# Modulation tiles among the gate groups, cosines from a magnitude, and a new order of low halves and head loads

## The reference, cut to what matters

```
# first block
proj = rms_norm(x) @ w_in                 # q, k, v, u, gate_a, gate_b
y_a  = windowed attention(q, k, v) @ w_attn_o
y_b  = state-space scan over u, both directions, then a gated linear unit (glu)
x    = x + (sigmoid(gate_a) * y_a + sigmoid(gate_b) * y_b) @ w_out
# experts: every token picks 8 x 16 of 16384 single-neuron experts
x    = x + sum over picked experts of weight * gelu(h . down[e]) * up[e]
# second block, for layer 0 and 1
shift, scale, gate = split(silu(c) @ w_mod[layer] + b_mod[layer], 3)      # and the same for c_ctx
x_in = x * (1 + scale) + shift
layer 0: short convolution and 8 latent attention heads;  layer 1: grouped attention
```

## Time and profile before

| | us |
|---|---|
| median of three runs | 4051.4 |
| the runs | 4050.02 to 4071.21 |
| the profiled execution | 4045.63 |
| its span | 4043.8 |
| TensorE's mean granted clock in it | 0.987 |

### The profile page before, as it was taken

The page is one execution under the profiler, slowest core; times in us unless marked ns, Lnnn a source line. Parts: engine busy times, 40 slices in busy tenths (PEclk is TensorE's granted clock), DMA queues, the critical chain, the costliest instruction groups (busy, mean ns, idle before and its releaser), DMA issues.

```text
span 4043.8 us, 73486 instructions
## 1 busy us (share of the span) xinstructions
PE 3846.4 (95%) x30344; PEld 3566.3 (88%) x30344; DVE 2409.5 (60%) x3400; ACT 1673.4 (41%) x2349; POOL 818.0 (20%) x599
## 2 busy tenths in 40 slices
PE   6999998899999988999999999999999999989997
PEld 6767677799999987999999999999799997778887
DVE  6999976543677767555555555533333333657556
ACT  4223345544455567333444334432222223243674
POOL 4878763234400000000000000000000002113223
PEclk9999999999999999999999999999999999999999
DMA  5777773245455544555655555522522223214323
GB/s 218 300 305 276 302 283 133 108 180 185 168 191 193 195 140 137 190 197 188 225 221 217 194 201 194 191 105 95 175 91 86 104 104 125 94 66 143 116 104 135
DMA packets 141589, 695.06 MB, mean 172 GB/s; under 512 B 44256, under 2 KB 54624, under 8 KB 61664
## 3 DMA queue, kind: packets, MB, share of 16 engines
q1 hardware_dynamic: 89952, 641.77, 43.2%
q10 hardware_dynamic: 51456, 50.74, 3.7%
HBM read 672.54 MB, written 19.92 MB: 171 GB/s over the span
## 4 chain that ended last, share of the span: by engine, by line
PE 77%; DVE 14%; ACT 3%; issue 3%; DMA 1%; POOL 1%; ACTq 0%; DVEq 0%; SPq 0%; POOLq 0%
PE banks L422 50%; PE banks L2231 17%; DVE w_lo L400 2%; PE banks L2299 1%; DVE pq L1340 1%; DVE banks L1330 1%; PE banks L2142 1%; PE banks L2401 1%; ACT w_hi L392 1%; DVE rq L1376 1%; DVE banks L1317 1%; DVE oh L1577 1%; PE banks L2467 1%; PE banks L2442 1%; POOL w_lo L400 1%
## 5 line engine op out<-in xcount | busy, mean ns | idle before, releaser
L422 PE MATMUL banks<-h_hi,w_hi 128*128 128x256 f32 (+1 forms) x6176 | 1640.7, 287 | 62.4 <-DVE w_lo L400 30.8
L422 PE MATMUL banks<-h_hi,w_lo 128*128 128x256 f32 (+1 forms) x6176 | 1617.3, 283 | 0.0
L422 PE MATMUL banks<-h_lo,w_hi 128*128 128x256 f32 (+1 forms) x6176 | 1616.9, 283 | 0.0
L392 ACT CAST w_hi<-ring 128x1024 fp32r<-128x1024 f32 x986 | 984.4, 1048 | 1041.3 <-PE banks L2231 427.5
L400 DVE TENSOR_TENSOR w_lo<-ring,w_hi 128x1024 fp32r<-128x1024 f32 x806 | 1000.8, 1274 | 559.7 <-ACT w_hi L392 555.2
L422 PEld LDWEIGHTS banks<-h_hi,w_hi 128*128 128x128 f32 x6176 | 1110.7, 189 | 126.3 <-issue 98.5
L422 PEld LDWEIGHTS banks<-h_hi,w_lo 128*128 128x128 f32 x6176 | 1109.4, 189 | 13.2 <-issue 0.5
L422 PEld LDWEIGHTS banks<-h_lo,w_hi 128*128 128x128 f32 x6176 | 1109.1, 189 | 11.8
L400 POOL TENSOR_TENSOR w_lo<-ring,w_hi 128x1024 fp32r<-128x1024 f32 x180 | 460.3, 2557 | 1628.9 <-ACT w_hi L392 1627.4
L2231 PE MATMUL banks<-wp_hi,w_hi 128*128 128x256 f32 x2048 | 566.3, 277 | 5.2 <-DVE wp_lo L1610 5.1
L2231 PE MATMUL banks<-wp_hi,w_lo 128*128 128x256 f32 x2048 | 566.1, 276 | 0.0
(11 more groups left out here) (388 smaller groups left out, 4307.3 us busy)
## 6 DMA issues: line engine op xcount, KB each, us to landing
ring<-in_stream_dram SPq DMA_DIRECT2D x555, 1024.0 KB, 4.8
spare<-in_stream_dram SPq DMA_DIRECT2D x30, 1024.0 KB, 5.9
cst<-in_stream_dram SPq DMA_DIRECT2D x23, 1024.0 KB, 6.7
g_in<-g_out ACTq DMA_DIRECT2D x8, 1024.0 KB, 6.4
g_out<-stage ACTq DMA_DIRECT2D x31, 256.0 KB, 2.6
hb<-heads_d ACTq DMA_DIRECT2D x8, 768.0 KB, 6.7
heads_d<-stg ACTq DMA_DIRECT2D x4, 1024.0 KB, 8.7
X<-in_x_in_dram SPq DMA_DIRECT2D x2, 1024.0 KB, 7.1
```

The source lines that it names most:

```text
L392: act.copy(w_hi[:, t.par, s], weights(t.slot)[:, s]).then_inc(hi_done, 1)
L422: m = pe.matmul(bank(b, e - a, a), w[:, t.par, k], x(k)[:, a:e], start=first and a == 0, stop=last and e == n, skip_group_check=e - a < n)
```

## The change

- Four modulation tiles an octet, 32 in all, leave the mixed stage and form the phase `gmod` behind `down0`. They run between the gate groups, one a group and two at four of them (`late_by`), with eight turns; their input and their copy use the place of constants that are loaded again afterwards. For that the gate groups use three sets of two banks, and bank 7 and 6 serve the late tiles. The groups' loops are written out.
- Cosines: VectorE rounds one phase only; ScalarE takes its magnitude and then the cosine as the sine of a quarter turn less the magnitude. The coefficients' last two instructions become one.
- Gate projections: GpSimd makes both low halves. Glu: VectorE makes both; the high split goes ahead of the exponentials, the first low half ahead of the wait for them.
- First up tile: its splits come behind the gate groups.
- Head loop: values are loaded by themselves; queries, keys and rotated queries of the next head are loaded once the present scores have been read.

```diff
-PHASES = [("u", 8), ("v", 4), ("mix", 136), ("gate", 12), ("glu", 16), ("attno", 16),
+PHASES = [("u", 8), ("v", 4), ("mix", 104), ("gate", 12), ("glu", 16), ("attno", 16),
-          ("down0", 64), ("up0", 64), ("down1", 64), ("up1", 64),
+          ("down0", 64), ("gmod", 32), ("up0", 64), ("down1", 64), ("up1", 64),
-SLOTS = [(D_, M_, M_), (M_, M_), (D_, M_), (D_, M_), (M_, M_), (D_, M_), (D_, M_), (M_, M_)]
+SLOTS = [(D_, M_), (M_,), (D_, M_), (D_, M_), (M_,), (D_, M_), (D_, M_), (M_,)]
+LATE = 16
-LAST = {4: G0["gate"], 5: G0["mix"] + MIX * 6 + 4, 6: G0["mix"] + MIX * 4 + 11}
+LAST = {4: G0["gate"], 5: G0["mix"] + MIX * 6 + 3, 6: G0["mix"] + MIX * 4 + 9}
...
-            b = 2 * (n % 4)
+            b = 2 * (n % 3)
+        def late_by(n):
+            return min(32, 32 * (n + 1) // 28)
...  ScalarE: tables
-                act.wait_ge(S("phs_ready"), c0 + 1)
-                act.activation(tab[c0 % 2][:], ph[:, 0:2], ACT.Sin, scale=TURN).then_inc(S("tab_ready"), 1)
+                act.wait_ge(S("phs_ready"), 2 * c0 + 1)
+                act.activation(ph[:, 1], ph[:, 0], ACT.Abs).then_inc(S("phs_ready"), 1)
+                act.wait_ge(S("phs_ready"), 2 * c0 + 2)
+                act.activation(tab[c0 % 2][:, 0], ph[:, 0], ACT.Sin, scale=TURN)
+                act.activation(tab[c0 % 2][:, 1], ph[:, 1], ACT.Sin, bias=V("halfpi"), scale=-TURN)\
+                    .then_inc(S("tab_ready"), 1)
...  ScalarE: glu
                 t = Tile("glu", h)
+                hi_split(act, t.next())
                 act.wait_ge(S("negmax_ready"), h + 1)
...
-                hi_split(act, t.next())
...  ScalarE: gate groups
-            with act.Fori(0, 7, 1) as i:
-                for n in range(4, 8):
-                    gates_weigh(n, i, 4)
-                    gates_stage(n - 2, i, 4)
-                    gates_store(n - 3, i, 4)
+            def late_out(b):
+                act.wait_ge(mm_done, Tile("gmod", 4 * (b - LATE) + 3).done())
+                act.wait_ge(S("mod_turned"), b)
+                act.copy(mtmp_late, bank(7)).then_inc(S("mod_out"), 1)
+            for n in range(2, 32):
+                gates_weigh(n)
+                gates_stage(n - 2)
+                if n >= 3:
+                    gates_store(n - 3)
+                while blocks < 24 and late_by(n - 1) >= 4 * (blocks - LATE + 1):
+                    late_out(blocks)
+                    blocks += 1
+            hi_split(act, Tile("up0", 0))
...  ScalarE: head loop
+                act.dma_start(hb[:, 0:2].unsqueeze(1), of_head(i)[:, :, 0:2]).then_inc(S("head_loaded"), 16)
...
+                act.dma_start(hb[:, 2:3].unsqueeze(1), of_head(i)[:, :, 2:3]).then_inc(S("values_loaded"), 16)
...
+                if more:
+                    scores_load(i + 1)
...  GpSimd
             for j in range(12):
-                lo_split(pool, Tile("gate", j).next(), 0)
-            for j in range(16):
-                lo_split(pool, Tile("glu", j).next(), 0)
+                for h_ in (1, 0):
+                    lo_split(pool, Tile("gate", j).next(), h_)
...  VectorE: phases and coefficients
-                L(dve.tensor_scalar(ph[:, 1], ph[:, 0], 0.25, None, ALU.add))
-                for f in range(2):
-                    L(dve.tensor_scalar(ph[:, 2], ph[:, f], MAGIC, MAGIC, ALU.add, ALU.subtract))
-                    m = dve.tensor_tensor(ph[:, f], ph[:, f], ph[:, 2], ALU.subtract)
+                L(dve.tensor_scalar(ph[:, 2], ph[:, 0], MAGIC, MAGIC, ALU.add, ALU.subtract))
+                dve.tensor_tensor(ph[:, 0], ph[:, 0], ph[:, 2], ALU.subtract).then_inc(S("phs_ready"), 1)
...
-                L(dve.tensor_tensor(ph[:, 0], ph[:, 0], ph[:, 1], ALU.add))
-                dve.tensor_scalar(co[:, :, 2], ph[:, 0], -1.0, None, ALU.mult).then_inc(S("c_made"), 1)
+                dve.scalar_tensor_tensor(co[:, :, 2], ph[:, 0], -1.0, ph[:, 1], ALU.mult, ALU.subtract)\
+                    .then_inc(S("c_made"), 1)
...  VectorE: gates, glu
-                lo_split(dve, Tile("gate", j).next(), 1)
...
+                lo_split(dve, t.next(), 1)
                 dve.wait_ge(S("exp_done"), h + 1)
...
-                lo_split(dve, t.next(), 1)
+                lo_split(dve, t.next(), 0)
...  VectorE: gate groups
+            for n in range(2, 32):
+                onehots(n)
+                scale(n - 2)
             scale(30)
             scale(31)
+            for h in (1, 0):
+                lo_split(dve, Tile("up0", 0), h)
...  TensorE
-                if v in (0, 2, 5) and q:
+                if v in (0, 5) and q:
                     pe.wait_ge(S("mix_read"), d)
                     mod_turn(q // 4 - 1)
...
-                    pe.wait_ge(S("gates_in"), g(-3))
-                    pe.wait_ge(S("g_staged"), g(-3))
+                    pe.wait_ge(S("gates_in"), g(-2))
+                    pe.wait_ge(S("g_staged"), g(-2))
...
+            def late_tile(j):
+                t = Tile("gmod", j)
+                if j % 4 == 0:
+                    pe.wait_ge(S("mod_out"), LATE + j // 4)
+                pe.wait_ge(tile_loaded[t.slot], t.loaded())
+                for r in range(4):
+                    m = pe.matmul(banks[32 * r:32 * r + 32, 7, :], csp_late[:, 4 * (j % 4) + r], weights(t.slot)[:, 4 * r:4 * r + 4],
+                                  start=(j % 4 == 0), stop=(j % 4 == 3))
+                m.then_inc(mm_done, 1)
+            for n in range(32):
                 gates_pe(n)
+                if turned < 24 and made >= 4 * (turned - LATE + 1):
+                    late_turn(turned)
+                    turned += 1
+                while made < late_by(n):
+                    if made % 4 == 0 and made // 4 + LATE > turned:
+                        late_turn(turned)
+                        turned += 1
+                    late_tile(made)
+                    made += 1
```

More of the change, by code:

```diff
@@ L725, in _ @@
             act.activation(sv[:], sv[:], ACT.Exp).then_inc(S("sel_acts"), 1)
-            with act.Fori(0, 16 - SELECT, 1) as i:
+            with act.Fori(0, 15 - SELECT, 1) as i:
                 for j in range(4):
@@ L730, in _ @@
                     down_act(t, i * 4 + (j + 4 * SELECT))
+            for j in range(60, 64):
+                t = Tile("down0", j)
+                if j < 63:
+                    hi_split(act, t.next())
+                down_act(t, j)
             act.sem_inc(S("sel_acts"), 1)
@@ L778, in _ @@
             gates_store(31)
+            act.wait_ge(S("mod_turned"), 24)
+            act.copy(modf[:, 8 * LATE:], bank(6, 64)).then_inc(S("mod_read"), 1)
             act.dma_start(C("rm"), consts[:, CONST["rm"][0]:CONST["rm"][0] + 1024]).then_inc(S("back"), 16)
             act.dma_start(C("rg"), consts[:, CONST["rg"][0]:CONST["rg"][0] + 512]).then_inc(S("back"), 16)
-            up_act(0)
+            for j in range(4):
+                hi_split(act, Tile("up0", j).next())
+            up_act(0, 1)
             act.wait_ge(mm_done, G0["down1"])
@@ L898, in _, with of_head, scores_load @@
             act.wait_ge(S("head_loaded"), 16)
[L900 to L904 removed]
+            def of_head(i):
+                return heads_d.rearrange("h p a t -> p h a t")[:, bass.ds(i, 1)]
+            def scores_load(i):
+                act.dma_start(hb[:, 0:2].unsqueeze(1), of_head(i)[:, :, 0:2]).then_inc(S("head_loaded"), 16)
                 for half in range(2):
@@ L907, in _, with conv_head @@
                                   rope_d.rearrange("h p t -> p h t")[:, bass.ds(i, 1)]).then_inc(S("head_loaded"), 16)
+            def conv_head(i, more=True):
+                tb, tc, tu, tg = (Tile("conv", j, i, 4) for j in range(4))
+                act.wait_ge(S("mpv_read"), at(1, i, 1))
+                act.dma_start(hb[:, 2:3].unsqueeze(1), of_head(i)[:, :, 2:3]).then_inc(S("values_loaded"), 16)
                 hi_split(act, tb.next())
@@ L928, in _ @@
                 act.activation(cvg[:], bank(tg.bank()), ACT.Silu).then_inc(S("cvg_ready"), 1)
+            scores_load(0)
+            with act.Fori(0, 7, 1) as i:
+                conv_head(i)
+            conv_head(7, more=False)
             def act_out(name, layer, n):
@@ L1393, in _ @@
                     heads_scaled(j // 2 - 1)
+                if j == 11:
+                    for h_ in range(2):
+                        dve.wait_ge(lo_done[h_], N0["glu"] + 1)
                 if j == 10:
                     dve.wait_ge(S("mod_read"), 1)
-                    for layer in range(2):
-                        L(dve.tensor_tensor(mods[:, layer], mods[:, layer],
-                                            V("bmod", 48 * layer, 48).unsqueeze(2).to_broadcast([P, 48, 2]), ALU.add))
+                    bias(0)
             dve.wait_ge(S("back"), 16)
@@ L2049, in mod_turn @@
                 for n in range(4):
-                    m = pe.matmul(bank(b // 3 % 2, 2, T + 8 * b + 2 * n), mtmp[:, n * P:(n + 1) * P], C("pick", 0, 2), start=True, stop=True)
```

(24 more changed lines are left out.)

70 lines of the change are left out of this document (33 added, 37 removed).

## The result

| | before | after | ratio |
|---|---|---|---|
| median of 7 runs each (us) | 4054.8 | 4090.4 | 1.0075 (95%: 1.0052 to 1.0098) |
| profiled execution (us) | 4045.6 | 4090.4 | |
| its span (us), mean TensorE clock | 4043.8, 0.987 | 4088.6, 0.975 | |

The forecast was 4044 us in 4005 to 4088. The time came out above the range, 0.75% slower. Rival A, with a chance of 0.18, had said 4091 us, worked out as net +40; the medians are 35.6 us apart and the profiled executions 44.8.

What follows compares the result with a forecast made beforehand. Bounds differ by stage (TensorE 95% busy overall, VectorE full in the mixed stage), with tiles expected to saturate the gate groups' DMAs. 4045.6 less 42 plus 35 gave 4038.6 us profiled, so a 4044 us median, range 4005 to 4088.

Steps and rivals of the forecast that it cites:

- Rival A: Gate groups: stores landing in 5.3 us behind tile transfers become the clock; +82 there, net +40, 4091 us; chance 0.18.
- Step 1: Mixed stage: shorter phase chain for cosines and coefficients gains 1.3 us an octet, 9 us in all (7 to 27).
- Step 2: Mixed stage: four modulation tiles fewer in each octet gain 7 us at the stage's end (0 to 10).
- Step 3: Gate projections: both low halves on GpSimd, two tiles in 13.9 us instead of 16.07; gain 14 us (5 to 17).
- Step 4: Glu and attention: earlier high splits and low halves on VectorE remove TensorE's 2.0 us wait; gain 11 us (3 to 16).
- Step 5: Head loop: a smaller first load shortens TensorE's one wait before the first head; gain 1 us (0 to 3).
- Step 6: Gate groups: the added modulation tiles cost 35 us, 29 for DMA and 6 for turns and boundary (10 to 85).
- B: Gate groups: transfers overlap better, so bytes bind and not engine time; net -25, 4026 us; chance 0.32.
- C: Gates and glu: the rearranged low halves gain nothing, gains fall by 17, net +10, 4061 us; chance 0.12.

Runs made afterwards that it cites:

- e1: The changed kernel with ScalarE's copy of bank 7 moved ahead of the high split and sine tables in the mixed stage; ratio 1.0045 to the kernel before.
- e4: The kernel before with every part of the change except the late tiles, which stay in the mixed stage; ratio 0.9888 to the kernel before.
- e5: The changed kernel with e1's moved copy and a third stage buffer in the gate groups; ratio 0.9994 to the kernel before.
- e10: e4 again, in more rounds, on one chip with e11; ratio 0.9866 to the kernel before, 4007.8 us against 4064.1.
- e6: The kernel before with only the low halves reordered in gate projections and glu; ratio 0.9895 to the kernel before.
- e3: The changed kernel with 28 of 32 late tiles loading only 64 KB of 1 MB, all matmuls and waits kept; ratio 0.9952 to the kernel before.
- e11: e6 again, in more rounds, on one chip with e10; ratio 0.9932 to the kernel before.
- e7: e4 with the gate projections' low halves as before, one half each on GpSimd and VectorE; ratio 0.9899 to the kernel before.
- e8: e4 with GpSimd making only 128 of 1024 columns of the low halves of gate tiles 4, 6, 8 and 10; one execution, 3992.0 us.

## Why the prediction was wrong

**Step 1 (cosines, -9): the edit did what was said, but the gain was lost to a wait that the change brought.** I priced each instruction on VectorE and each tile on TensorE, and never followed ScalarE's new order: the copy behind the tables. The prediction wrote that ScalarE's extra work "lies in its idle time". Its busy time does; what stands behind it in program order does not. e1 shows 1.5 us an octet (61.15 to 59.65) where step 1 had 1.3, with four tiles fewer in it.

**Step 2 (fewer tiles, -7): not seen.** The changed kernel's stage ends 3.5 us later. After 490 us VectorE no longer waits for high halves beyond 1.8 us (8.3 before), so what step 2 saw went, but TensorE's waits for the copy of bank 7 took its place. e4 reaches nearly the octets of e1 with all tiles in place. With the copy moved the first gate tile came at 574.7 (e1) and 571.5 us (e5), against 579.8 in e4; but e10, the same kernel as e4, had it at 567.2, so no run shows a gain of step 2 beyond the spread of one kernel. Its price of a tile on TensorE was also half of the true one (see step 6).

**Step 3 (gate projections, -14): 9.2.** Between the reciprocals nothing was gained (15.8 us, not 13.9; 0.4 us lost over the three gaps), since the scalings, "1.7" in the prediction, take 4.7 beside GpSimd. The 6.5 us of the prediction also counted all three gaps at 16.07, where the third took 14.8 already; and 668.2 is the end of the scalings, while the last reciprocal ended at 666.5. The way to the first reciprocal gave 6.2 us, the way from the last one to glu 3.4. The stretched rounding of the earlier trace rows showed the same effect; I used it in step 1 and did not carry it to step 3.

**Step 4 (glu, -11): right in kind, small by 2.** 12.8 us measured for 11 (8.7 in e4, 15.7 in e6), two heads in 16.7 us, the low halves' wait gone.

**Step 5 (head loads, -1): open.** Up to the first head the changed kernel took 7.2 us less, and its wait fell from 8.1 to 1.5 us, yet e4 and e10 with the same head loads wait 7.8 and 7.5 us. So the gain hangs on how stores and loads meet there, not on the loads' order alone.

**Step 6 (gate groups, +35): the step that failed.** Two terms of it were mis-sized. The transfers (+29) were priced as engine time, as if full DMA engines were the bound and a store's latency free; the measured landing of 5.3 us with two buffers made the store the clock, at a DMA share of 0.80. This is 54.6 us by e3, the slower clock of TensorE included. And the matrix work, which was to "just fit", was taken at half its size: 1.04 us a tile for 0.53, and e3's stage is 19 us longer than before with next to no loads. The turns' waits for ScalarE's copy, taken at 4 us, were 9.0 (5 waits).

**The rivals.** Rival A gave a landing of 5.3 us, and 5.3 was measured; its period of 5.6 came out as 169.5/32 = 5.3. Its point of decision, a landing grown by 1.3 us, was passed twice over. What spoke against it (a small store, one tile a group) did not weigh: the median landing doubled, so most stores met a load. The chance of 0.18 was too low for a chain that the prediction itself had found without slack (2.6 of 2.87 us). That 4091 met the 4090.4 so closely is partly luck. A had the gate groups at +82 and the other gains at 42; measured were 73.6 and 28.8, and of the 73.6 the 19 that e3 leaves are not A's mechanism. The two errors nearly cancel. The Trainium skill, page "DMA: Bandwidth & Descriptors", section "Queues, rings and completion order", has each DMA engine take turns between the rings of the issuing queues. The trace agrees with it in direction: the landing doubled beside 1 MB loads and stayed at 2.6 us beside 64 KB ones. B did not happen. Of C, GpSimd's instances did not stretch in the gates; VectorE's scalings did.

## What to carry to other kernels

Before bandwidth is called idle and filled, look for a transfer in the same stretch whose landing is already part of a cycle without slack: its latency, not its share of the engines, sets the price, and more buffers buy back only a part. When an edit puts instructions on an engine with idle time, follow what is queued behind it, since the idle engine's order can still stop a full one; and when TensorE waits, read its granted clock behind the wait, since that time comes on top. Count a tile's instructions from a whole stage (records divided by tiles), not from a piece of a chain.

## What the runs showed of the hardware

**A stretch of slower matmuls at full granted clock.** In 6 of the 13 profiled executions TensorE runs some 4% slower for 200 us or more, while its clock reads 1.00 and other engines keep their durations. The window 2300 to 2400 us of the kernel before, and of e6, in the same code:

```profile
2300.00:2400.00 100.00, 100.00 (x885) 100.00 (x884) 56.29 (x75) 37.27 (x38) 0.00 (x0) 1.00 0.57 211
```
```profile
2300.00:2400.00 100.00, 100.00 (x851) 100.00 (x850) 53.68 (x72) 35.50 (x36) 0.00 (x0) 1.00 0.54 190
```

A matmul there takes 281 ns instead of 276, 851 start where 885 did. e6 shows it from about 2250 us on, e11 between 1050 and 1400, e4 from about 1950; the profiled executions of before, after and e10 have none in up and down. Up and down to the first head took 1365 to 1366 us in e4, e6 and e7, and 1351 in e10. What slows it stays open. This is why stages of several profiles are compared above, and ends only by their intervals.

**Two instructions stretched by GpSimd.** Scalings of 0.48 and 1.28 us take 1.4 and 3.4 beside GpSimd's low halves, and are back at 0.48 and 1.28 where GpSimd makes none at that moment (e7, e8).
